# A two-block transformer on one core: order of block-diagonal projections, gate rows, value evictions and halvings in the setup of a matrix memory

## What is computed

```python
def mlstm_branch(u, o_pre, i_pre, f_pre, conv_w, conv_b, w_q, w_k, w_v, b_i, b_f, norm_g):
    c = jax.nn.silu(causal_dwconv(u, conv_w, conv_b))
    q = block_diag(c, w_q)
    k = block_diag(c, w_k) * (ML_HEAD_DIM ** -0.5)
    v = block_diag(u, w_v)
    ig = i_pre + b_i
    fg = f_pre + b_f
    h = mlstm_chunkwise(q, k, v, ig, fg)
    ...
```

## Time and profile before

| What | Value |
|---|---|
| Median of three runs | 3410.78 us |
| Profiled execution, its own time | 3404.92 us |
| Its span | 3402.9 us |
| TensorE busy | 3233.2 us (95%) |
| VectorE busy | 2338.9 us (69%) |
| ScalarE busy | 1837.9 us (54%) |
| Layer 0: gate rows, og and mu | about 172 to 240 us |
| Layer 0: mq, mk, mv | about 236 to 265 us |
| Layer 1: the same two | about 854 to 931 and 926 to 955 us |

### The profile page before, as it was taken

One profiled execution on the slowest core, in us unless ns is written; L12 is line 12 of the kernel. 1 busy time (PEld: TensorE's weight loads), 2 busy tenths in 40 slices (PEclk: granted clock), 3 DMA queues, 4 the chain that ended last, 5 costly groups with the idle time before them and its releaser, 6 DMA issues.

```text
span 3402.9 us, 56025 instructions
## 1 busy us (share of the span) xinstructions
PE 3233.2 (95%) x24147; PEld 2990.3 (88%) x24147; DVE 2338.9 (69%) x2994; ACT 1837.9 (54%) x2184; POOL 0.2 (0%) x4
## 2 busy tenths in 40 slices
PE   8999999999889899999999999989899989999898
PEld 7988999999889799999999999878678889985698
DVE  6876655567766588888888888755574556465455
ACT  5464544455644377777777777643464444344443
POOL 0000000000000000000000000000000000000000
PEclk9999999999989999999999999999899999999999
DMA  6432565454334689999899999632323466530353
GB/s 254 166 141 99 179 235 199 156 192 164 124 112 161 236 343 361 337 357 358 338 356 357 336 358 354 249 135 75 112 86 147 141 232 242 215 129 24 138 188 121
DMA packets 102812, 723.62 MB, mean 213 GB/s; under 512 B 11424, under 2 KB 13344, under 8 KB 16672
## 3 DMA queue, kind: packets, MB, share of 16 engines
q1 hardware_dynamic: 102560, 719.97, 57.4%
HBM read 718.87 MB, written 1.05 MB: 212 GB/s over the span
## 4 chain that ended last, share of the span: by engine, by line
PE 77%; DVE 12%; ACT 8%; issue 2%; DMA 1%; SPq 0%; DVEq 0%; ACTq 0%
PE PS L1548 13%; PE PS L1549 13%; PE PS L1550 13%; PE PS L1499 6%; PE PS L1501 6%; PE PS L1500 6%; DVE WL L2270 4%; ACT WH L1880 3%; PE PS L1816 3%; PE PS L1817 3%; PE PS L1818 3%; PE PS L1659 2%; PE PS L1630 2%; PE PS L1603 1%; PE PS L1647 1%
## 5 line engine op out<-in xcount | busy, mean ns | idle before, releaser
L2270 DVE TENSOR_TENSOR WL<-RAW,WH 128x2048 fp32r<-128x2048 f32 (+2 forms) x428 | 963.0, 2252 | 561.1 <-ACT WH L1880 556.0
L1880 ACT ACTIVATE WH<-RAW 128x2048 fp32r<-128x2048 f32 (+2 forms) x428 | 803.2, 1880 | 246.4 <-PE PS L1550 184.8
L1548 PE MATMUL PS<-PH,WH 128*128 128x256 f32 x2464 | 710.7, 288 | 41.1 <-DVE PL L2474 7.8
L1549 PE MATMUL PS<-PL,WH 128*128 128x256 f32 x2464 | 700.9, 284 | 0.0
L1550 PE MATMUL PS<-PH,WL 128*128 128x256 f32 x2464 | 700.5, 284 | 0.0
L2270 DVE TENSOR_TENSOR WL<-F,WH 128x2048 fp32r<-128x2048 f32 x210 | 480.6, 2289 | 79.8 <-ACT WH L1880 79.2
L1548 PEld LDWEIGHTS PS<-PH,WH 128*128 128x128 f32 x2464 | 473.4, 192 | 48.6 <-issue 32.2
L1548 PE MATMUL PS<-HPH,WH 128*128 128x256 f32 (+1 forms) x1648 | 490.1, 297 | 16.9 <-ACT WH L1880 8.7
L1549 PE MATMUL PS<-HPL,WH 128*128 128x256 f32 (+1 forms) x1648 | 478.1, 290 | 0.0
L1550 PE MATMUL PS<-HPH,WL 128*128 128x256 f32 (+1 forms) x1648 | 477.5, 290 | 0.0
L1549 PEld LDWEIGHTS PS<-PL,WH 128*128 128x128 f32 x2464 | 473.7, 192 | 0.8
(11 more groups left out here) (393 smaller groups left out, 4982.5 us busy)
## 6 DMA issues: line engine op xcount, KB each, us to landing
F<-in_moe_w SPq DMA_DIRECT2D x210, 1024.0 KB, 6.1
RAW<-in_ffn_w SPq DMA_DIRECT2D x130, 1024.0 KB, 5.0
RAW<-in_moe_w SPq DMA_DIRECT2D x126, 1024.0 KB, 6.2
RAW<-in_w_in SPq DMA_DIRECT2D x64, 1024.0 KB, 4.9
F<-in_ada_w SPq DMA_DIRECT2D x18, 1024.0 KB, 11.3
RAW<-in_w_kv SPq DMA_DIRECT2D x16, 1024.0 KB, 4.9
G<-in_ada_w SPq DMA_DIRECT2D x15, 1024.0 KB, 9.0
RAW<-in_w_in_ab SPq DMA_DIRECT2D x12, 1024.0 KB, 5.0
```

Of the source, the lines that this page charges most:

```text
L1548: T_.matmul(out, lh, rh, start=first, stop=False)
L1549: T_.matmul(out, lh, rl, start=False, stop=False)
L1880: S.activation(mem["WH"][:, t.s % NHL, 0:m], v.raws[t.slot][:, 0:m], ACT.Copy).then_inc(*ac.done("w_hi", t.s))
L2270: V.tensor_tensor(mem["WL"][:, t.s % NHL, 0:m], v.raws[t.slot][:, 0:m], mem["WH"][:, t.s % NHL, 0:m].bitcast(F32), sub).then_inc(*dv.done( ...
```

## The change

It has five parts. The gate rows are copied out with their bias by two ScalarE activations in a new unit `rowin`, put right behind `if`, which frees the bank; VectorE's row step 0 reads the copies. The row chain first waits for the planner's busy time of VectorE. The drain before mq no longer flushes `cva` and `cvd` of mu's last blocks. mq and mk are interleaved: blocks 0 to 5 of both, then 6 and 7 of both, with tiles split two ahead instead of three. The last row's Exp becomes a unit `rowout` behind mk. mv's odd blocks are emptied by ScalarE; its tile unit comes ahead of the pair of yrg, and the pair of xa comes after the first branch tile.

```diff
+        if g.evac == "vdtok":
+            return ((A, 0.3),) if i % 2 else ((V, 0.35),)
...
-    def drain(self, lanes=2, fill=False, then=None):
+    def drain(self, lanes=2, fill=False, then=None, flush=True):
 
-        self.soon(True)
+        if flush:
+            self.soon(True)
...
         p.put("if", l)
+        p.freed_at["if", l] = p.put("rowin", l, after=p.clock)
 
         def rows(l=l):
+            yield p.busy[V]
             for step in range(8):
                 yield p.put("row", l, step, after=p.clock) + 0.3
...
         p.lanes = 2
-        p.drain()
+        p.drain(flush=False)
         u = [("cv_lo", f"mu{l}", 7)]
         p.fgc = ALL
-        p.lin_all(L("mq", "diag", "f32", io["ml_w_q"][l], 0, 256, p2, ready=u, dst="F5"))
-        p.lin_all(L("mk", "diag", "f32", io["ml_w_k"][l], 0, 256, p2, ready=u, dst="F6"))
+        twins = [L("mq", "diag", "f32", io["ml_w_q"][l], 0, 256, p2, ready=u, dst="F5"),
+                 L("mk", "diag", "f32", io["ml_w_k"][l], 0, 256, p2, ready=u, dst="F6")]
+        for blocks in (range(6), range(6, 8)):
+            for g in twins:
+                if blocks[0] == 0:
+                    p.begin(g, 0)
+                    p.open(g, 0, 2)
+                for i in blocks:
+                    p.block(g, 0, i)
+        p.put("rowout", l)
+        mv = L("mv", "dtok", "vdtok", io["ml_w_v"][l], 0, 256, p1, ready=u)
+        p.begin(mv, 0)
+        p.open(mv, 0, 2)
         p.put("pair", f"yrg{l}")
-        p.lin_all(L("mv", "dtok", "vdtok", io["ml_w_v"][l], 0, 256, p1, ready=u))
-        p.put("pair", f"xa{l}")
+        for i in range(8):
+            p.block(mv, 0, i)
...
                 p.lin(bs, t)
+                if br == 0 and t == 0:
+                    p.put("pair", f"xa{l}")
...
+        elif kind == "vdtok" and i % 2:
+            ac.wait_ge("ps", name, i)
+            S.activation(F[0][:, 4 + i // 2, :], ps, ACT.Copy).then_inc(*ac.done("free_a", name, i))
...
+    def rowin(l):
+        rw, ps = v.rw, bank(("if", l))
+        ac.wait_ge("ps", "if", l)
+        S.activation(rw[0], ps[0:4, 0:T], ACT.Identity, bias=v.rows(2 * l))
+        S.activation(rw[3], ps[32:36, 0:T], ACT.Identity, bias=v.rows(2 * l + 1)).then_inc(*ac.done("free_a", "if", l))
+
     def row(l, step):
         if step == 0:
             ac.wait_ge("rows_e", l)
             S.activation(v.rw[2], v.rw[2], ACT.Exp).then_inc(*ac.done("rows_x", l))
-        elif step == 7:
-            ac.wait_ge("rows", l, "m")
-            S.activation(v.rw[4], v.rw[4], ACT.Exp, scale=-1.0).then_inc(*ac.done("rows_em", l))
+
+    def rowout(l):
+        ac.wait_ge("rows", l, "m")
+        S.activation(v.rw[4], v.rw[4], ACT.Exp, scale=-1.0).then_inc(*ac.done("rows_em", l))
...
-            elif kind == "vdtok":
+            elif kind == "vdtok" and i % 2 == 0:
...
         if step == 0:
-            ps = bank(("if", l))
-            dv.wait_ge("ps", "if", l)
             dv.wait_ge("rgy", l, 7)
-            V.tensor_scalar(rw[0], ps[0:4, 0:T], v.rows(2 * l), None, add)
-            V.tensor_scalar(rw[1], ps[32:36, 0:T], v.rows(2 * l + 1), None, add).then_inc(*dv.done("free_d", "if", l))
-            dv.wait_ge("free_d", "if", l)
-            dv.turn(V.tensor_scalar(rw[2], rw[1], -1.0, None, mult))
-            V.tensor_tensor(rw[2], rw[2], rw[1], mn).then_inc(*dv.done("rows_e", l))
+            dv.wait_ge("free_a", "if", l)
+            V.tensor_copy(rw[1], rw[3])
+            dv.turn(V.tensor_scalar(rw[2], rw[3], -1.0, None, mult))
+            V.tensor_tensor(rw[2], rw[2], rw[3], mn).then_inc(*dv.done("rows_e", l))
```

More of the change, by code:

```diff
@@ L277, in work @@
     if kind == "row":
-        return (((V, 1.5), (A, 0.4)), ((V, 2.3),), ((V, 2.1),), ((V, 1.7),), ((V, 1.7),), ((V, 2.5),), ((V, 1.2),), ((V, 2.6), (A, 0.4)))[args[1]]
+        return (((V, 1.5), (A, 0.4)), ((V, 2.3),), ((V, 2.1),), ((V, 1.7),), ((V, 1.7),), ((V, 2.5),), ((V, 1.2),), ((V, 2.6),))[args[1]]
     if kind == "napp":
@@ L294 @@
     "rope2": ((V, 1.2),), "mga": ((A, 0.33),), "mgd": ((V, 0.4),), "h2a": ((A, 0.33),), "h2d": ((V, 0.35),), "pair": ((A, 1.85), (V, 2.21)),
-    "yml": ((A, 0.55), (V, 0.6)), "adac": ((A, 0.5),), "turned": ((V, 0.25),), "acol": ((V, 0.1),), "gains": ((V, 0.2),),
+    "yml": ((A, 0.55), (V, 0.6)), "adac": ((A, 0.5),), "turned": ((V, 0.25),), "acol": ((V, 0.1),), "rowin": ((A, 0.6),), "rowout": ((A, 0.4),), "gains": ((V, 0.2),),
 }
@@ L1712, in ml @@
             pe.wait_ge("free_d", "ml", l, hd, 1)
-            pe.freed((f"mv{l}", 7))
+            for i in (6, 7):
+                pe.freed((f"mv{l}", i))
             for s_ in range(2):
@@ L2193, in lam2 @@
         S.activation(mem["LVS"][:, 2:4], mem["LVS"][:, 0:2], ACT.Exp).then_inc(*ac.done("lam2_e"))
-    do = {"start": start, "lam": lam, "tile": tile, "lin": lin, "nsq": nsq, "nmid": nmid, "napp": napp, "cva": cva, "e": e, "t": t, "v": vv, "sub0": sub0, "sub2": sub2, "rgc": rgc, "row": row,
+    do = {"start": start, "lam": lam, "tile": tile, "lin": lin, "nsq": nsq, "nmid": nmid, "napp": napp, "cva": cva, "e": e, "t": t, "v": vv, "sub0": sub0, "sub2": sub2, "rgc": rgc, "rowin": rowin, "row": row, "rowout": rowout,
           "ml": ml, "pair": pair, "yml": yml, "mga": mga, "h2a": h2a, "adac": adac, "rtop": rtop, "tt": tt, "gather": gather, "up": up, "turn": turn,
```

## The result

The changed kernel took 3376.3 us (median of 4 runs, 3370.7 to 3380.5) against 3411.4 for the kernel before: a ratio of 0.9902, 95% interval 0.9889 to 0.9916. The medians lie 35 us apart, and the interval stands for 29 to 38. In a second set on one chip it was 3377.1 against 3409.1 (0.9907, 0.9890 to 0.9923). The prediction was 3382, from 3368 to 3400.

What follows compares the result with a forecast made beforehand. TensorE, busy 95%, was taken as the bound, its waits and half clock worth at most 38.3 us. Layer 0's 12.3 plus layer 1's 18.6 less 2.3 gave 28.6 us: 3376.3 profiled, median 3382, range 3368 to 3400.

Steps and rivals of the forecast that it cites:

- Part 1: Layer 1's og/mu stretch: gate rows copied out by ScalarE free the bank early, 7.5 us won (bounds 4 to 10.7).
- the 7.38 us go in full: Layer 1's fourth score: TensorE's whole 7.38 us wait for the gate rows' PSUM bank disappears.
- 7 us of usable gaps: VectorE in layer 1's og/mu stretch: of some 12.8 us of gaps, about 7 are usable early.
- The rival that VectorE becomes the bound: VectorE has hardly a gap from mq on; layer 1's first part returns 4, total gain 12.4 us, 3398; chance 0.20.
- Part 2: Layer 0's og/mu blocks: later row steps let holes of 2.96 us close, 2.0 us won (bounds 0 to 2.96).
- Parts 3 and 4 without xa's halving: Setup from mq to first gate: block order, later Exp, value evictions on both engines win 10.3 and 11.1 us by layer.
- The table switch: ScalarE before the first gate: Exp's table load costs its 1.28 us without a further pause; rival with pause, chance 0.04.
- xa's halving, 2.3 us lost: Memory stretch: halving moved behind the first branch tile costs 2.3 us in all (bounds -11 to +11).
- the same 3.9 us wait at the memory's third head: Expected sign: TensorE's 3.9 us wait for a memory step at the third head stays.
- The rival of a shift that does nothing (2): Row steps don't move, step 0 still blocks ScalarE's queue; 2.0 and some 3 us go, 3387; chance 0.07.
- the slower one (5): Memory heads: late halving and evictions stall every head's round, six new stalls, 33 us, 3427; chance 0.04.
- a new wait on a memory step behind 265: Sign the forecast would be wrong: new TensorE waits on memory steps after 265 us; no size given.

Runs made afterwards that it cites:

- e1: Kernel before plus only the ScalarE copies of the gate rows; row steps and order as before: ratio 1.0003.
- e9: Changed kernel with early row steps and gate rows copied out by VectorE again: 3368.6 us, ratio 0.9882.
- e7: Changed kernel with the last gate row's Exp back in row step 7: 3381.9 us, ratio 0.9913.
- e8: Changed kernel with xa's halving one tile of the first branch later still: 3394.3 us, ratio 0.9949.
- e6: Changed kernel with row steps as early as in the kernel before, rows still copied by ScalarE: 3369.6 us, ratio 0.9879.
- e12: Changed kernel, unaltered, run once more on another chip: 3377.1 us, ratio 0.9907.
- e3: Kernel before plus only interleaved mq/mk blocks, no flush of mu's last convolutions, and the last row's Exp behind mk: ratio 0.9974.
- e10: Changed kernel with xa's halving back behind the values and the fourth memory head begun 3 us later in the planner: 3390.5 us, ratio 0.9949.

## Why the prediction came out as it did

The forecast named 28.6 us for the profiled execution's parts; the cuts gave 33.4. By its own steps:

- **Part 1, 7.5 us: wrong, nothing.** The step that failed is "the 7.38 us go in full". I had seen ScalarE wait 10.29 us at the Exp of the row step and called its queue blocked, but took only the bank for the cause of TensorE's wait. Freed of the bank, TensorE met the same blocked queue at og's bank, 7.48 us (e1), and e9 has the original wait back at no cost. I had looked for the next late thing on VectorE's convolutions and given 7 us of usable gaps. What was late was og's eviction and the splits behind ScalarE's Exp. The 0.9 us that layer 1's first cut did gain were a loss of 0.4 in the second profile. The rival that VectorE becomes the bound is nearer, since that Exp waits for VectorE's recurrence and splits, though it left 4 us. The Trainium skill (Perfetto Trace Analysis, Optimization Strategies) advises to speed up the engines that block the critical path. The runs agree only if the blocking thing is taken as the instruction at the head of the queue: e1 took two additions of 0.47 us off VectorE for a copy of 0.28, and a bank wait off TensorE, and the time stayed.
- **Part 2, 2.0 us: wrong, and of the other sign, 1.9 lost in layer 0.** My lower bound was 0, with a loss excluded for no reason. The shifted steps landed in the og and mu blocks, and ScalarE's evictions and splits came later: one hole of 3.36 us in place of 1.65 and 1.30, with 1.7 of half clock behind (4.00 x 0.43). The clock is most of that loss, and it is partly chance: with the same hole at full clock e7 and e8 lose 0.2. It also costs the 0.8 at mq's first bank that I named as its price (0.87 measured) in both layers. Together e6 is 7.5 us under the second set of the changed kernel, on another chip; by the cuts against e12 it is 4.5.
- **Parts 3 and 4 without xa's halving, 10.3 and 11.1 us: right, 9.2 and 10.5.** First eviction 0.8 late, 0.87 measured; first gate from a bank that ScalarE frees, 0.5 late, 1.09 measured; the first gate 18.6 us after mq's start, 19.2 measured; clock 1.00 all through. They are not independent, which the split into two terms hid: block order alone gives 2.9 and 3.5 (e3), as the gate then waits 6.84.
- **The table switch: right, no pause.** ScalarE of the changed kernel before the gate:

```profile
251.58 1.28 ACT L2085 ACT_TABLE_LOAD   x1
252.87 0.42 ACT L2085 ACTIVATE R<-R 4x256 f32<-4x256 f32 x1
253.20 1.90 ACT L1899 ACTIVATE WH<-RAW 128x2048 fp32r<-128x2048 f32 x1
255.00 1.90 ACT L2112 ACTIVATE PH<-F 128x2048 fp32r<-128x2048 f32 x1
256.81 1.15 ACT L1965 ACTIVATE F<-PS 128x256 f32<-128x256 f32 x4
```

  The Exp begins 0.01 us behind the load's end, and everything to the value evictions follows without a gap. The Trainium skill's drain of 1.38 us beside a load (ScalarE: Activation LUTs, What ACT_TABLE_LOAD costs) shows no pause here either, ahead of the load (251.18 and 0.38 of L1957 to 251.58) or behind it; by it the first gate would have waited 1.4 us more than my 0.5, and it waited 0.6 more.
- **xa's halving, 2.3 us lost: wrong, 14.7 gained.** I had bounded it from +11 to -11 and then took its plain length, with "the same 3.9 us wait at the memory's third head" among what was to be seen. Both layers have 1.7 there, at full clock. What I had not read in the kernel before is the order of the small products and the splits in VectorE's queue, which its timeline shows at 318.44. That order accounts for at most two thirds of the gain (in layer 0 2.2 us of wait and 2.3 of lower clock, of 7.0). The rest is three waits of 0.8 to 1.4 us from 342.98 on that are one of 1.14, and why xa's place decides over them is open.

So 28.6, less 6.5 for part 1, 3.9 for part 2 and 1.7 for parts 3 and 4, and 17.0 more for xa, is 33.5. That the number lies in the range is luck: an error of 17 us in one direction met three of 12 together in the other.

The rival of a shift that does nothing (2) did not come, and neither did the slower one (5). Its condition, new stalls at the memory heads, is what e8 and e10 show for one head, 6.1 and 6.9 us. Of the signs of being wrong one came, a new wait on a memory step behind 265: the 1.14 us at the fourth head, in both layers.

## What to carry to other kernels

Removing a wait that names a bank won nothing here, as another engine's queue was blocked and TensorE met it at the next bank. So ask which instruction stands at the head of each engine's queue during the wait, and what the waiting engine would need next. Where a queue is in program order, read what stands between a small dependent pair (an exponential and its product): a long weight split with its own wait for the other engine, caught between them, went with TensorE's longest waits in the memory here, and moving an unrelated halving by one tile put it there or took it away. Edits that shorten consecutive waits are best tried together as well as alone, as the first can move its gain to the next (e3). Before a gain is put down to an edit, compare the granted clock behind the same wait in more than one execution.

## What the runs showed beside that

Identical instructions took 2293 to 2306 us in the rest of the kernel, and most of the difference lies in a few stretches where one execution is granted a lower clock than another. Windows at the same places behind layer 1's first load of w_out, of the changed kernel:

```profile
2108.10:2338.10 230.00, 213.59 (x1356) 0.96 0.39 144
2913.10:3028.10 115.00, 110.78 (x839) 0.96 0.39 140
```

of e10:

```profile
2123.60:2353.60 230.00, 213.69 (x1363) 0.99 0.39 144
2928.60:3043.60 115.00, 110.73 (x869) 1.00 0.40 142
```

and of the kernel before:

```profile
2141.40:2371.40 230.00, 213.55 (x1350) 0.96 0.39 142
2946.40:3061.40 115.00, 110.75 (x860) 0.99 0.38 137
```

A share of 0.02 to 0.03 over 230 us is 5 to 7, and 0.04 over 115 is 5: together most of the 12.5 us between e10's rest and that of the changed kernel. The two switch independently (before: low, high; e9: high, low; e10: both high; changed: both low). They are not all: the second profile of the changed kernel is low in both too, and its rest is 3.6 us shorter than the first's. That the same makes the runs of one kernel differ by 10 to 13 us is likely but not shown, as only one or two of them were profiled. Where there is one profiled execution of each kernel, a gain of under 10 us is read from its own stretch, not from the span.
